# The first stage multiplies half of the GLA gate columns before the shift is known; the GLA groups run with five tiles

## The chip, the core and the metric

The kernel runs on one core of one Trainium2 chip. The metric is device time in microseconds (us), the median of several runs. Lower is better. TensorE multiplies, VectorE and ScalarE prepare its operands, GpSimd computes small reciprocal roots, SyncE (SP) issues the loads.

## What is computed

One hybrid layer for 512 tokens of width 2048, all in float32. Its six modulation rows come from the conditioning row `c`:

```python
mod = (c_act @ w_ada[i] + b_ada[i])[:, None, :]
shift_m, scale_m, gate_m, shift_f, scale_f, gate_f = jnp.split(mod, N_MOD, axis=-1)
h = rmsnorm(x, g_pre_mix[i]) * (1.0 + scale_m) + shift_m
y = token_mixer(h, ...)            # inside: proj = h @ w_in
fq, fk, fv, ff, gq, gk, gv, ga, gr = jnp.split(proj, IN_OFFSETS, axis=-1)
...
gla = head_rmsnorm(gla, g_gla_out).reshape(b, s, GLA_WIDTH) * jax.nn.silu(gr)
```

`w_in` has 2048 rows. Its columns feed eight attention heads (FoX, 128 wide, queries, keys and values), four linear-attention heads (GLA, keys 128, values 256, gate `gr` 256 wide each) and 24 small columns (`ff`, `ga`). An output projection and a squared-ReLU network of hidden width 8192 follow; the change leaves them alone.

## The kernel before

**Precision.** A float32 product is made of three fast matmuls (`split_mm`, L775): each operand is split into a rounded part (`_hi`, a copy on ScalarE) and a rest (`_lo`, a subtraction on VectorE), and hi x hi, hi x lo and lo x hi are summed in PSUM. A plain float32 matmul (L813) needs no split operands, and takes longer.

**Groups.** The input projection is cut into eight groups: four FoX groups of two heads and four GLA groups of one head. Each has `TILES` = 6 tiles of 128 output columns by 512 tokens, one PSUM bank each, and runs over KT = 16 k-tiles of 128 rows (`group_steps`, L781). The operand `h`, transposed, stays in `in_hi` and `in_lo`; in a GLA group the tiles are GQ, GK, GV0, GV1, GR0 and GR1, the last two being the two halves of the head's gate. The weights come two k-tiles at a time into two slots `w_raw`, are split into `w_hi` (L1207) and `w_lo` (L1640), and the slot's next load waits for both (`slot_free`, L503). While group r is multiplied, the small work of group r-1 is done in slots between the tiles (`fox_slot`, `gla_slot`); in four of the groups VectorE also sums the modulation columns of the second half of the layer (`f_item`, L1690). At the end of a group ScalarE copies tiles 0, 2 and 4 and VectorE tiles 1, 3 and 5 from PSUM to `grp`.

**The first stage.** Before group 0 can run, `scale_m` and `shift_m` have to be summed from 32 MB of `w_ada`. VectorE multiplies each k-row block with its `c_act` value and adds it to `am_acc` (`add_am`, L1869): 32 items of 1 MB. An item holds scale and shift columns of the same k-tiles of `h`; the table `BLOCKS` makes three blocks of four k-tiles (8 items, operations 1024 wide) and two blocks of two (4 items, 512 wide). At a block's end TensorE sums `am_acc` over the partitions with a row of ones (L981, `start_slot`), VectorE turns the sums into `mod_a` and `mod_b` (`mod_columns_m`, L1906), and ScalarE modulates the k-tile and rounds it (`modulate`, L1345: `in_tmp` L1347, `in_hi` L1350); VectorE makes `in_lo` (L1897). k-tiles 2, 3, 6 and 7 (`WHOLE`) are multiplied as plain float32, from `w_raw` and `in_tmp`. The 40 small columns (`misc_step`, L986) are multiplied at the places that `FILL_AT` names. Before all this, ScalarE squares and scales the four x tiles, TensorE transposes them (L965) and ScalarE copies them to `xn_t` (L1339).

**Queues.** Each engine works its instructions in the order in which they are written. SP issues all loads of the stage in one row (L620 to L640): four item slots, so item n waits until item n-4 is used.

**Between group 0 and 1.** The small columns give the forget gates: VectorE L1973 to L1976, ScalarE Exp and Ln with a table load (L1367, L1369), and only then ScalarE's evictions of group 0 (L1218).

Of the kernel before, what the change touches and what calls it, by code (L numbers as in the profile page):

```python
# [35 lines left out]
F32 = mybir.dt.float32  # L36
# [5 lines left out]
P = 128  # L42
# [3 lines left out]
def build_block(nc, x, c, w_ada, b_ada, g_pre_mix, g_post_mix, w_in, b_fgate, w_gla_a2, b_gla_a2,  # L46
# [30 lines left out]
    GQ, GK, GV0, GV1, GR0, GR1 = range(6)  # L77
    MM_G = KT // 2
# [19 lines left out]
    F_USED = len(ITEMS)  # L98
# [14 lines left out]
    with ExitStack() as ctx:  # L113
# [39 lines left out]
        am_item = [at(f"am_item{s}", [P, 2, 2, 512], (R_AD, R_AD + 8 * KIB, R_G, R_G + 8 * KIB)[s]) for s in range(4)]  # L153
        am_acc = [at(f"am_acc{s}", [P, 2, 512], (R_T + 12 * KIB, R_GG + 4 * KIB)[s]) for s in range(2)]
# [4 lines left out]
        wm_hi = at("wm_hi", [P, KT, 40], R_GG, F32R)  # L159
# [48 lines left out]

        acc = small("acc", [P, 2 * P])
# [16 lines left out]
        decay = small("decay", [P, NCH])  # L226
        assert k_at[0] <= nc.sbuf_usable_end
# [33 lines left out]

        hi_done = sem("hi_done")
# [8 lines left out]
        rows_tr = sem("rows_tr")  # L271
        c_tr = sem("c_tr")
        cols_ready = sem("cols_ready")
        ce_ready = sem("ce_ready")
        c_ready = sem("c_ready")
# [2184 lines left out]
```

## Time and profile before

| | |
|---|---|
| time, median of 3 runs | 2235.53 us (2233.84 to 2235.6) |
| profiled execution, span from first to last instruction | 2231.3 us |
| around the span (median less span) | 4.2 us |
| TensorE busy | 2171.6 us, 97% |
| VectorE busy | 1508.8 us, 68% |
| ScalarE busy | 868.1 us, 39% |
| GpSimd busy | 376.0 us, 17% |
| granted TensorE clock, mean | 0.993 |
| moved by DMA | 441.17 MB, mean 198 GB/s |

The profile is of one execution; its own time is the span and what lies around it, here taken from the median. A row of the timeline has the start, the duration, engine, line, operation, what it writes and reads, how often, and in brackets the idle time of the engine before it with what ended it. The durations of matmuls overlap: what counts is the distance of their starts. Records of a plain float32 matmul come in twos.

### The profile page before, as it was taken

The page shows a single profiled execution, that of the slowest core. Times are in us where ns is not written, and L with a number is a line of the kernel's source. Part 1 is how long each engine was busy: PE and PEld are TensorE (multiplying, and loading weights), DVE is VectorE, ACT ScalarE, POOL GpSimd, SP SyncE. Part 2 cuts the span into 40 slices and gives each one's busy share as a digit, 9 for nine tenths or more (in the row PEclk, how much of TensorE's full clock was granted, in tenths as well). Part 3 has the DMA queues.
Part 4 walks back from the last instruction along what each step waited for, and adds up shares of the span by engine and source line. Part 5 has one row for each costly group of instructions (what it writes and reads, how often), then busy time and mean ns, then how long its engine had stood idle before and what let it go on. Part 6 is the DMA issues. An engine that isn't in the chain of part 4 may idle for free.

```text
span 2231.3 us, 26551 instructions
## 1 busy us (share of the span) xinstructions
PE 2171.6 (97%) x9835; PEld 1765.5 (79%) x9835; DVE 1508.8 (68%) x1485; ACT 868.1 (39%) x1096; POOL 376.0 (17%) x207
## 2 busy tenths in 40 slices
PE   4989999999999999999999999999999999999998
PEld 3568888887777888888888888888878888888886
DVE  6877666666767634664355445544689889898998
ACT  5233333331333223533344335334443444343443
POOL 1000000000000001100000000000035545463645
PEclk9999999999999999999999999999999999999999
DMA  9956554753554353565666656746364765567663
GB/s 363 355 181 215 196 178 142 237 162 113 159 170 137 108 195 101 182 220 215 206 205 220 222 173 205 240 174 203 132 207 170 244 227 169 190 234 244 239 230 147
DMA packets 266403, 441.17 MB, mean 198 GB/s; under 512 B 18156, under 2 KB 118704, under 8 KB 260280
## 3 DMA queue, kind: packets, MB, share of 16 engines
q1 hardware_dynamic: 265472, 435.45, 58.1%
q10 hardware_dynamic: 824, 4.27, 0.5%
q8 instruction: 70, 1.15, 0.2%
q14 instruction: 37, 0.30, 0.0%
HBM read 379.88 MB, written 59.79 MB: 197 GB/s over the span
## 4 chain that ended last, share of the span: by engine, by line
PE 85%; issue 8%; DVE 4%; DMA 1%; ACT 1%; SPq 1%; POOL 0%; DVEq 0%; POOLq 0%; ACTq 0%
PE pair L777 27%; PE pair L779 27%; PE pair L778 26%; DVE am_acc L1880 2%; DMA am_item<-in_w_ada 1%; PE pair L886 1%; PE pair L860 1%; DVE v_op L2165 0%; PE pair L877 0%; PE pair L981 0%; PE pair L926 0%; PE pair L935 0%; PE pair L827 0%; SPq L607 0%; POOL rstd L2330 0%
## 5 line engine op out<-in xcount | busy, mean ns | idle before, releaser
L777 PE MATMUL pair<-in_hi,w_hi 128*128 128x512 f32 (+1 forms) x1800 | 719.6, 400 | 9.2 <-DVE in_lo L2073 3.8
L779 PE MATMUL pair<-in_hi,w_lo 128*128 128x512 f32 (+1 forms) x1800 | 697.2, 387 | 0.0
L778 PE MATMUL pair<-in_lo,w_hi 128*128 128x512 f32 (+1 forms) x1800 | 696.2, 387 | 0.0
L1640 DVE TENSOR_TENSOR w_lo<-w_raw,w_hi 128x2048 fp32r<-128x2048 f32 (+1 forms) x139 | 289.5, 2083 | 395.5 <-ACT w_hi L1207 395.1
L1207 ACT ACTIVATE w_hi<-w_raw 128x2048 fp32r<-128x2048 f32 (+1 forms) x141 | 243.4, 1726 | 466.1 <-PE pair L779 404.8
L777 PEld LDWEIGHTS pair<-in_hi,w_hi 128*128 128x128 f32 x1800 | 339.4, 189 | 88.6 <-issue 20.1
L779 PEld LDWEIGHTS pair<-in_hi,w_lo 128*128 128x128 f32 x1800 | 338.8, 188 | 70.2
L778 PEld LDWEIGHTS pair<-in_lo,w_hi 128*128 128x128 f32 x1800 | 339.6, 189 | 67.6 <-issue 2.6
L777 PE MATMUL pair<-v_op,hid_r 128*128 128x512 f32 x896 | 349.0, 390 | 2.1 <-issue 0.9
L779 PE MATMUL pair<-v_op,hid_r 128*128 128x512 f32 x896 | 348.6, 389 | 0.0
L778 PE MATMUL pair<-v_op,hid_r 128*128 128x512 f32 x896 | 348.6, 389 | 0.0
L2165 DVE TENSOR_TENSOR v_op<-v_raw,v_op 128x1024 fp32r<-128x1024 f32 x192 | 302.3, 1595 | 64.8 <-ACT v_op L1613 63.6
L1613 ACT ACTIVATE v_op<-v_raw 128x1024 fp32r<-128x1024 f32 x192 | 203.3, 1061 | 287.1 <-PE pair L779 269.0
L2409 POOL TENSOR_TENSOR v_sum<-v_raw,v_raw 128x512 f32<-128x512 f32 x60 | 149.2, 2513 | 364.1 <-DVE v_raw L2180 364.1
L777 PEld LDWEIGHTS pair<-v_op,hid_r 128*128 128x128 f32 x896 | 168.2, 188 | 38.9 <-issue 3.2
L779 PEld LDWEIGHTS pair<-v_op,hid_r 128*128 128x128 f32 x896 | 168.2, 188 | 34.9
L778 PEld LDWEIGHTS pair<-v_op,hid_r 128*128 128x128 f32 x896 | 168.2, 188 | 34.8
L2418 POOL TENSOR_TENSOR v_raw<-v_raw,v_sum 128x512 f32<-128x512 f32 x60 | 135.3, 2284 | 18.4 <-DVE v_op L2165 18.4
L2336 POOL TENSOR_TENSOR ada<-ada,c_act 128x2048 f32<-128x2048 f32 x8 | 29.8, 3721 | 592.3 <-DMA ada<-in_w_ada 555.0
L2215 DVE TENSOR_TENSOR y_t<-pair,y_t 128x1024 f32<-128x1024 f32 x104 | 125.0, 1215 | 0.3 <-PE pair L779 0.3
L777 PE MATMUL pair<-w_hi,in_hi 128*128 128x512 f32 x256 | 101.3, 396 | 0.0
L778 PE MATMUL pair<-w_lo,in_hi 128*128 128x512 f32 x256 | 99.7, 389 | 0.0
(218 smaller groups left out, 1928.9 us busy)
## 6 DMA issues: line engine op xcount, KB each, us to landing
w_raw<-in_w_mlp_in SPq DMA_DIRECT2D x64, 1024.0 KB, 5.3
v_raw<-in_w_mlp_out SPq DMA_DIRECT2D x128, 512.0 KB, 4.9
hid_r<-hid_scratch SPq DMA_DIRECT2D x112, 512.0 KB, 6.3
hid_scratch<-hid_r SPq DMA_DIRECT2D x28, 1792.0 KB, 7.9
am_item<-in_w_ada SPq DMA_DIRECT2D x64, 512.0 KB, 7.6
w_raw<-in_w_in SPq DMA_DIRECT2D x128, 256.0 KB, 3.5
af_item<-in_w_ada SPq DMA_DIRECT2D x64, 512.0 KB, 4.5
w_raw<-in_w_in SPq DMA_DIRECT2D x128, 128.0 KB, 3.6
```

The source lines that it names most:

```text
L777: pe.matmul(dst, a[0], b[0], start=start, stop=False, skip_group_check=onto)
L778: pe.matmul(dst, a[0], b[1], start=False, stop=False, skip_group_check=onto)
L779: return pe.matmul(dst, a[1], b[0], start=False, stop=stop, skip_group_check=onto)
L1207: act.activation(w_hi[n][:, view], w_raw[n][:, view], ACT.Copy).then_inc(hi_done, 1)
L1613: act.activation(v_op[i % 4][:, 0, :], raw_of(u, p)[:, h, :], ACT.Copy).then_inc(v_hi, 1)
L1640: dve.tensor_tensor(w_lo[n][:, view], w_raw[n][:, view], w_hi[n][:, view].bitcast(F32), ALU.subtract)\
L1880: last = dve.scalar_tensor_tensor(total, item, c_k, total, ALU.mult, ALU.add)
L2165: dve.tensor_tensor(v_op[i % 4][:, 1, :], raw_of(u, p)[:, h, :], v_op[i % 4][:, 0, :].bitcast(F32), ALU.subtract).then_inc(v_lo, 1)
L2215: return dve.tensor_tensor(dst, src[:, :, :], dst, ALU.add)
L2336: pool.tensor_tensor(unit[:, :, :], unit[:, :, :], c_act[:, :].rearrange("p (k o) -> p k o", o=1).to_broadcast([P, KT, P]), ALU.mult)\
L2409: last = pool.tensor_tensor(v_sum[:, h, cols], v_raw[q[B22]][:, h, cols], v_raw[q[B11]][:, h, cols], ALU.add)
L2418: last = pool.tensor_tensor(b21, b21, v_sum[:, h, cols], ALU.subtract)
```

## The change

The 128 columns of GR1 of all four GLA heads (512 columns of `w_in`) are taken out of the GLA groups, which then have `GLA_TILES` = 5 tiles. They are multiplied in the first stage, as four plain float32 tiles per k-tile, from `in_tmp` = `xn_t` times `mod_a` alone, that is with the scale and without the shift (`fill_operand`, `fill_w`). The results are parked in `gg`. The shift's share is the same for all tokens: the sum over k of `mod_b` times the weight. For this the same columns are loaded again in the four FoX groups, four k-tiles in each (`load_gr`), VectorE sums them into `gr_acc` (`gr_step`), and TensorE makes the column sums at the end of the last FoX group (`f_columns` with `gates`). When a GLA group is evicted, VectorE adds the parked tile and this column (`evict_gla`).

So the items are cut otherwise: first 16 items of the scale, then 16 of the shift, each with four k-rows of 512 columns, so that all operations are 512 wide. The k-tiles in plain float32 are gone from group 0, and so is `FILL_AT`: the small columns follow the tiles of their k-tile. The x tiles are loaded before the first item.

```diff
+    GLA_TILES = TILES - 1
...
-    BLOCKS = ((0, 4), (4, 4), (8, 4), (12, 2), (14, 2))
-    M_BLOCKS = len(BLOCKS)
-    ITEMS = [(b, i) for b, (_, nk) in enumerate(BLOCKS) for i in range(2 * nk)]
+    S_BLOCKS = KT // 4
+    M_BLOCKS = 2 * S_BLOCKS
...
             def load_am(n):
                 if n >= 4:
                     sp.wait_ge(am_used, n - 3)
+                block, i = divmod(n, 4)
+                col = (SCALE_M, SHIFT_M)[block // S_BLOCKS] + block % S_BLOCKS * 512
+                for half in range(2):
+                    k = 4 * i + 2 * half
+                    sp.dma_start(am_item[n % 4][:, 2 * half:2 * half + 2, :], w_ada_t[:, k:k + 2, col:col + 512])\
                         .then_inc(am_in[n % 4], 16)
...
+            for t in range(TB):
+                load_x(t)
+            for n in range(16):
                 load_am(n)
+                if n % 2 == 0:
+                    load_fill(n // 2)
             load_fox(0, 0, wait=False)
+            load_wm(0)
+            for n in range(16, 20):
+                load_am(n)
             load_fox(0, 1, wait=False)
+            load_wm(1)
...
+            for n in range(20, 32):
                 load_am(n)
+                if n % 2 and n < 28:
+                    load_fox(0, (n - 17) // 2)
...
+                    if mm == 1:
+                        load_gr(r - 1)
```

TensorE:

```diff
+            for k in range(KT):
+                if k % 4 == 0:
+                    sum_columns(k // 4)
+                    pe.wait_ge(fill_in[k // 4], 64)
+                pe.wait_ge(fill_tmp, k + 1)
+                for h in range(GLA_HEADS):
+                    last = pe.matmul(bank[h][:, :], fill_w[k // 2][:, k % 2, h, :], in_tmp[:, k, :],
+                                     start=(k == 0), stop=(k == KT - 1))
+                    if k == KT - 1 or k % 2 and h == GLA_HEADS - 1:
+                        last.then_inc(fill_used, 1)
+            sum_columns(S_BLOCKS)
+
+            SUM_AT = {7: S_BLOCKS + 1, 14: S_BLOCKS + 2, 22: S_BLOCKS + 3}
...
-            group_steps(FOX_GROUPS, False, fox_slots(FOX_GROUPS - 1))
+            group_steps(FOX_GROUPS, False, fox_slots(FOX_GROUPS - 1, gates=True), GLA_TILES)
             with pe.Fori(0, GLA_HEADS - 1) as h:
-                group_steps(h + (FOX_GROUPS + 1), False, lambda s: gla_slot(s, h))
+                group_steps(h + (FOX_GROUPS + 1), False, lambda s: gla_slot(s, h), GLA_TILES)
```

ScalarE:

```diff
+            for k in range(KT):
+                fill_operand(k)
             first_hi(0)
+            gate_hi(0)
+            for h in range(GLA_HEADS):
+                act.wait_ge(fill_used, MM_G + h)
+                act.activation(gg[:, h * 512:h * 512 + 512], bank[h][:, :], ACT.Copy).then_inc(fill_park, 1)
             for k in range(KT):
                 modulate(k)
+                if k == 1:
+                    first_hi(1)
+                    gate_hi(1)
+                elif k % 2 and k < KT - 1:
+                    split_hi((k + 1) // 2, arrived_group(0, (k + 1) // 2), (k + 1) // 2 % 2, group_view)
```

VectorE:

```diff
+            for block in range(S_BLOCKS):
+                for i in range(4):
+                    add_am(4 * block + i)
+                mod_columns(block)
+            first_lo(0)
+            add_am(16)
+            gate_lo(0)
+            for n in range(17, 20):
+                add_am(n)
+            mod_columns(S_BLOCKS)
...
+            for block in range(1, S_BLOCKS):
+                n, k = 4 * (S_BLOCKS + block), 4 * block
+                if block == 1:
+                    add_am(n)
+                    add_am(n + 1)
+                split_lo(2 * block, 0, group_view)
+                add_am(n + 2)
+                add_am(n + 3)
+                mod_columns(S_BLOCKS + block)
+                modulated_lo(k)
+                modulated_lo(k + 1)
+                split_lo(2 * block + 1, 1, group_view)
+                if block + 1 < S_BLOCKS:
+                    add_am(n + 4)
+                modulated_lo(k + 2)
+                modulated_lo(k + 3)
+                if block + 1 < S_BLOCKS:
+                    add_am(n + 5)
...
+            def gr_step(f, j):
+                dve.drain()
+                if j == 0:
+                    dve.wait_ge(gr_in, f * 64 + 64)
+                dve.scalar_tensor_tensor(gr_acc[:, :], gr_item[:, j, :], mod_b[:, bass.ds(f * 4 + j, 1)], gr_acc[:, :],
+                                         ALU.mult, ALU.add).then_inc(gr_used, 1)
...
+                    if b == GR1:
+                        dve.wait_ge(fill_park, GLA_HEADS)
+                        dve.tensor_scalar(grp[:, b, :], gg[:, bass.ds(h * 512, 512)], v_col[:, bass.ds(h, 1)], None,
+                                          ALU.add).then_inc(ev_dve, 1)
```

The order of TensorE's row behind the transposes of x, in the kernel before: the column sums (`ones,am_acc`), then the first k-tile in three parts.

```order
L965 MATMUL pair<-ident,x_raw 128x128 x3
L981 MATMUL pair<-ones,am_acc_86 128x1 [waits am_used,xt_act]
L981 MATMUL pair<-ones,am_acc_86 128x1 x7
L777 MATMUL pair<-in_hi,w_hi_76 128x512 [waits mod_lo,lo_done,hi_done]
L778 MATMUL pair<-in_lo,w_hi_76 128x512
L779 MATMUL pair<-in_hi,w_lo_78 128x512
```

The same place in the changed kernel, to the second of eight sums.

```order
L978 MATMUL pair<-ones,am_acc_86 128x1 [waits am_used,xt_act]
L978 MATMUL pair<-ones,am_acc_86 128x1 x3
L989 MATMUL pair<-in_tmp,fill_w_88 128x512 [waits fill_tmp,fill_in0]
L989 MATMUL pair<-in_tmp,fill_w_88 128x512 x3
L989 MATMUL pair<-in_tmp,fill_w_88 128x512 [waits fill_tmp]
L989 MATMUL pair<-in_tmp,fill_w_88 128x512 x3
...
L978 MATMUL pair<-ones,am_acc_87 128x1 [waits am_col,am_used]
L978 MATMUL pair<-ones,am_acc_87 128x1 x3
```

Where the split matmuls began, 16 plain tiles now stand, then the next sum; the split matmuls begin behind the fifth sum.

VectorE's row from the sum of one shift block to the next, in the changed kernel (`am_acc` sums of items, `w_lo` and `in_lo` rests).

```order
L1977 TENSOR_TENSOR mod_b<-pair,cols_a 128x4 [waits am_sum]
L1949 TENSOR_TENSOR in_lo<-in_tmp,in_hi 128x512 [waits mod_hi] x2
L1673 TENSOR_TENSOR w_lo_79<-w_raw_75,w_hi_77 128x1536 [waits w_used,hi_done]
L1936 TENSOR_SCALAR am_acc_86<-am_item_82,c_act 128x512 [waits am_sum,am_in0]
L1934 SCALAR_TENSOR_TENSOR am_acc_86<-am_item_82,c_act,am_acc_86 128x512 x3
L1949 TENSOR_TENSOR in_lo<-in_tmp,in_hi 128x512 [waits mod_hi] x2
L1934 SCALAR_TENSOR_TENSOR am_acc_86<-am_item_83,c_act,am_acc_86 128x512 [waits am_in1]
L1934 SCALAR_TENSOR_TENSOR am_acc_86<-am_item_83,c_act,am_acc_86 128x512 x3
L1673 TENSOR_TENSOR w_lo_78<-w_raw_74,w_hi_76 128x1536 [waits w_used,hi_done]
```

Behind these come two more items and the wait for the next sum. All item operations are now 512 wide, and both w_lo of a block stand between two sums.

TensorE's row at the last k-tile of group 0, before: the 40 small columns (`wm_hi`) ahead of the six tiles, of which the first is shown.

```order
L777 MATMUL pair<-in_hi,wm_hi 40x512 [waits mod_lo]
L778 MATMUL pair<-in_lo,wm_hi 40x512
L779 MATMUL pair<-in_hi,wm_lo 40x512
L777 MATMUL pair<-in_hi,w_hi_77 128x512
L778 MATMUL pair<-in_lo,w_hi_77 128x512
L779 MATMUL pair<-in_hi,w_lo_79 128x512
```

And in the changed kernel: the last tile, the small columns, and the first tile of group 1.

```order
L790 MATMUL pair<-in_hi,w_hi_77 128x512
L791 MATMUL pair<-in_lo,w_hi_77 128x512
L792 MATMUL pair<-in_hi,w_lo_79 128x512
L790 MATMUL pair<-in_hi,wm_hi 40x512
L791 MATMUL pair<-in_lo,wm_hi 40x512
L792 MATMUL pair<-in_hi,wm_lo 40x512
L790 MATMUL pair<-in_hi,w_hi_76 128x512 [waits ev_act,lo_done,hi_done]
```

The small columns have moved from before the six tiles to behind them.

## Rows read from the trace of the kernel before

**Rows 1.** The page, part 1: busy us (share of the span), instructions.

```profile
PE 2171.6 (97%) x9835; PEld 1765.5 (79%) x9835; DVE 1508.8 (68%) x1485; ACT 868.1 (39%) x1096; POOL 376.0 (17%) x207
```

**Rows 2.** Stretches: length, busy us of each engine, TensorE's granted clock, DMA share, GB/s.

```profile
40.00:50.00 10.00, 7.08 (x22) 5.81 (x22) 7.50 (x10) 5.46 (x8) 0.00 (x0) 0.51 1.09 359
60.00:70.00 10.00, 5.83 (x16) 2.37 (x14) 6.82 (x6) 1.84 (x2) 0.00 (x0) 1.00 1.08 355
200.00:220.00 20.00, 20.00 (x96) 16.05 (x95) 14.74 (x35) 6.88 (x12) 1.10 (x2) 1.00 0.57 184
520.00:540.00 20.00, 20.00 (x96) 15.90 (x96) 16.91 (x25) 3.58 (x3) 1.02 (x1) 1.00 0.28 79
```

**Rows 3.** Timeline of TensorE: start, duration, line, operation, [idle before].

```profile
27.37 9.79 PE L965 MATMUL pair<-ident,x_raw 128*128 128x128 f32 x64 [16.21 <-ACT x_raw L1327]
38.71 2.80 PE L981 MATMUL pair<-ones,am_acc 128*128 128x1 f32 x16 [1.55 <-DVE am_acc L1880]
44.43 0.76 PE L777 MATMUL pair<-in_hi,w_hi 128*128 128x512 f32 x1 [2.92 <-DVE in_lo L1897]
...
55.18 10.46 PE L813 MATMUL pair<-in_tmp,w_raw 128*128 128x512 f32 x24
69.81 3.20 PE L981 MATMUL pair<-ones,am_acc 128*128 128x1 f32 x16 [4.17 <-DVE am_acc L1880]
...
103.00 0.47 PE L777 MATMUL pair<-in_hi,w_hi 128*128 128x512 f32 x1 [0.81 <-DVE in_lo L1897]
...
137.78 0.95 PE L981 MATMUL pair<-ones,am_acc 128*128 128x1 f32 x8
...
142.31 0.40 PE L777 MATMUL pair<-in_hi,w_hi 128*128 128x512 f32 x1
...
146.42 0.40 PE L777 MATMUL pair<-in_hi,wm_hi 128*40 128x512 f32 x1
...
147.11 0.39 PE L777 MATMUL pair<-in_hi,w_hi 128*128 128x512 f32 x1
```

**Rows 4.** Timeline of VectorE in the first stage, the same columns.

```profile
22.23 16.33 DVE L1880 SCALAR_TENSOR_TENSOR am_acc<-am_item,c_act,am_acc 128x1024 f32<-128x1024 f32 x12 [4.50 <-DMA am_item<-in_w_ada]
...
102.17 0.68 DVE L1897 TENSOR_TENSOR in_lo<-in_tmp,in_hi 128x512 fp32r<-128x512 f32 x1
...
111.12 1.75 DVE L1640 TENSOR_TENSOR w_lo<-w_raw,w_hi 128x1536 fp32r<-128x1536 f32 x1
...
117.32 0.48 DVE L1882 TENSOR_SCALAR am_acc<-am_item,c_act 128x512 f32<-128x512 f32 x1
117.88 2.40 DVE L1880 SCALAR_TENSOR_TENSOR am_acc<-am_item,c_act,am_acc 128x512 f32<-128x512 f32 x3
```

**Rows 5.** Timeline of ScalarE in the first stage.

```profile
6.43 0.18 ACT L1322 ACTIVATE c_act<-pair 128x16 f32<-128x16 f32 x1
...
16.97 1.91 ACT L1333 ACTIVATE x_junk<-x_raw 128x2048 f32<-128x2048 f32 x1 [1.27 <-DMA x_raw<-in_x]
...
100.59 0.81 ACT L1347 ACTIVATE in_tmp<-xn_t,mod_b,mod_a 128x512 f32<-128x512 f32 x1 [10.58 <-DVE mod_a L1918]
```

**Rows 6.** Timeline from group 0 to group 1, three engines.

```profile
147.31 0.74 DVE L1973 TENSOR_SCALAR f_z<-pair,b_fg 8x512 f32<-8x512 f32 x1 [0.40 <-PE pair L779]
...
152.18 1.58 ACT L1218 ACTIVATE grp<-pair 128x512 f32<-128x512 f32 x3
...
152.92 0.47 PE L777 MATMUL pair<-in_hi,w_hi 128*128 128x512 f32 x1 [1.54 <-ACT grp L1218]
```

**Rows 7.** Waits of TensorE from 140 to 820 us: all there are.

```profile
PE pair L777 <- ACT grp L1218: 1.5, 1, 1.5
```

**Rows 8.** Timeline at a GLA group's start: its second pair of weights.

```profile
558.10 1.49 ACT L1207 ACTIVATE w_hi<-w_raw 128x1536 fp32r<-128x1536 f32 x1 [5.80 <-DMA w_raw<-in_w_in]
...
559.62 1.76 DVE L1640 TENSOR_TENSOR w_lo<-w_raw,w_hi 128x1536 fp32r<-128x1536 f32 x1 [2.51 <-ACT w_hi L1207]
...
562.45 0.48 PE L777 MATMUL pair<-in_hi,w_hi 128*128 128x512 f32 x1
```

More of the change, by code:

```diff
@@ L260, in build_block @@
         out_done = sem("out_done")
+        fill_in = [sem(f"fill_in{b}") for b in range(S_BLOCKS)]
+        fill_tmp = sem("fill_tmp")
+        fill_used = sem("fill_used")
+        fill_park = sem("fill_park")
+        gr_in = sem("gr_in")
+        gr_used = sem("gr_used")
         hi_done = sem("hi_done")
@@ L640, in _ @@
-            load_fox(0, MM_G - 1, first=True)
+                if n % 2 and n < 28:
+                    load_fox(0, (n - 17) // 2)
+            for mm in range(6, MM_G):
+                load_fox(0, mm)
             def load_cumb(f):
@@ L779, in split_mm, with group_steps @@
                 return pe.matmul(dst, a[1], b[0], start=False, stop=stop, skip_group_check=onto)
-            def group_steps(r, first, slot, misc_step=None):
+            def group_steps(r, first, slot, tiles, misc_step=None):
                 for k in range(KT):
@@ L804, in group_steps @@
-                    for b in range(TILES):
-                        if k == 0 and not first:
+                        pe.wait_ge(mod_lo, k + 1)
+                    for b in range(tiles):
+                        if k == 0 and first and b < GLA_HEADS:
+                            pe.wait_ge(fill_park, b + 1)
+                        elif k == 0 and not first:
                             pe.wait_ge((ev_act, ev_dve)[b % 2], r * 3 - 2 + b // 2)
                         cols = slice(b * P, b * P + P)
-                        if by_parts:
-                            last = split_mm(bank[b][:, :], (hi[:, cols], lo[:, cols]),
-                                            (in_hi[:, k, :], in_lo[:, k, :]), k == 0, k == KT - 1)
-                        else:
-                            last = pe.matmul(bank[b][:, :], raw[:, cols], in_tmp[:, k, :], start=False, stop=False)
-                        if k == KT - 1 and b < TILES - 1:
+                        last = split_mm(bank[b][:, :], (hi[:, cols], lo[:, cols]),
+                                        (in_hi[:, k, :], in_lo[:, k, :]), k == 0, k == KT - 1)
+                        if k == KT - 1 and b < tiles - 1:
@@ L824, in f_columns @@
+                    if first:
+                        misc_step(k)
+                    else:
+                        slot(2 * k + 1)
+            def f_columns(f, gates=False):
+                if gates:
+                    pe.wait_ge(gr_used, KT)
+                    for h in range(GLA_HEADS):
+                        pe.matmul(BA[:, 8 + h:9 + h], gr_acc[:, h * P:h * P + P], ones[:, 0:1], start=True, stop=True)
                 pe.wait_ge(am_used, f * F_ITEMS + (F_USED + F_ITEMS))
@@ L1389, in _, with group @@
             CAT_AT = {4 * (k // 2 + 1) + 2 + k % 2: k for k in range(12)}
-            def group(r, work, last=False):
+            def group(r, work, view, last=False):
                 for s in range(4 * MM_G):
@@ L1875, in add_am @@
                     dve.wait_ge(am_sum, block - 1)
-                for k in range(ks.start, ks.stop):
-                    item, c_k = item_view(n)[:, k - ks.start, :, :], c_act[:, k:k + 1]
-                    if k:
+                for j in range(4):
+                    item, c_k = am_item[n % 4][:, j, :], c_act[:, 4 * i + j:4 * i + j + 1]
+                    if i or j:
                         dve.drain()
@@ L1994, in _, with group @@
             CAT_AT = {4 * (k // 2 + 1) + 2 + k % 2: k for k in range(12)}
-            def group(r, work, last=False):
+            def group(r, work, view, last=False):
                 for s in range(4 * MM_G):
```

434 lines of the change are left out of this document (190 added, 244 removed).

## The prediction

> **What bounds the kernel now.** I read the page's busy times first, then stretches of 10 and 20 us, then the first 160 us engine by engine, then the waits behind them. TensorE is busy 97% of the span [rows 1], and from 200 to 220 us in every microsecond at full clock [rows 2]. After the first stage the trace shows one wait of TensorE up to 820 us, 1.5 us long [rows 7]. So every matmul taken out of the head groups is worth its full spacing, unless the shorter group uncovers a wait. The first stage is different: the DMA engines are full there (share 1.08 to 1.09, some 355 GB/s), TensorE is busy 5.8 of 10 us in one stretch [rows 2], and it waits for column sums that VectorE has to finish first (4.17 us in front of the sum at 69.81) [rows 3]. The stage ends where group 1 starts, at 152.92 us [rows 6].
>
> **Prices.** One k-step of six tiles in three parts (18 matmuls) goes from 142.31 to 146.42: 4.11 us, 0.685 a tile; the 40-column step beside it takes 0.69, so a step of the first stage costs 4.80 [rows 3]. A full-precision tile: two k-steps are 12 tiles, which the trace shows as 24 records in 10.46 us, 0.872 a tile [rows 3]. A four-column sum takes 0.95 at full clock and, by half of the 3.20 for eight, 1.6 at half clock [rows 3]; I take 1.8 with its start. VectorE: a 1024-wide product-sum has a pitch of 1.36 (12 in 16.33), a 512-wide one 0.82 (3 in 2.40), the first of a block 0.48 plus a gap; a w_lo 1.75, an in_lo 0.68 [rows 4]. So an item of 1 MB costs 2.7 us in the old form and 3.3 (3.0 for the first of a block) in the new one: 32 items take about 104 us where 20 wide and 12 narrow ones took 92. ScalarE: 0.81 for a modulation [rows 5], and less for the rounding copy behind it.
>
> The Trainium skill ("VectorE: DVE Perf Modes", the errata section) says that each instruction pays a fixed extra, and that tiles of 512 elements or more hide it. An estimate by its add formula makes four 512-wide operations 0.3 us dearer than two 1024-wide ones; the rows say 0.6. By the page the stage would lose half as much to the narrower items.
>
> **The first stage, step by step.**
> 1. Start. The x tiles go ahead of the items. The third x tile, now the third MB instead of the fifth, no longer makes ScalarE wait at 16.97; its eight passes of 1.9 to 2.0 us then run without a gap from 6.6, behind its first operation [rows 5]. The transposes start near 23.0 instead of 27.37, and the first sum, 11.3 us after them as now [rows 3], at 34.3. Gain 4.4. Items 0 to 3 are summed by about 31.6.
> 2. The fill. Four blocks, each: sum 0.95, VectorE's columns and ScalarE's operand about 1.35 (0.47 and 0.81, and hand-overs), then 16 full-precision tiles, 13.95. A block takes 16.25; four take 65.0, to 99.3. VectorE works 12.9 of each 16.25 us and then stands at its wait for the sum, so it can't run ahead.
> 3. The hand-over to the shift half. VectorE is let go by the fourth sum at about 84.5. Next in its row is the first w_lo, and ScalarE copies w_hi only behind four fill operands: 88.9. Then 1.7 for w_lo, 0.45 for the gate part, 13.0 for items 16 to 19: 104.0. TensorE has waited 4.7 us. Sum 1.8, shift columns 0.2, modulation, in_lo: the first split matmul starts at about 108.3 (44.43 now).
> 4. Sixteen k-steps of 4.80: 76.8. Whole k-tiles are gone: four k-steps fall from 5.23 to 4.11. Three sums, 5.4.
> 5. Waits in that half. Between two sums VectorE has four items (13.0), two w_lo (3.5), four in_lo (2.7), 19.4 in all, and stands idle for the sum and modulation after each sum (about 3.4), and for a w_hi that waits until TensorE has released the slot (1 to 3.4). That is 24 to 27 us a block against TensorE's 20.1. Walked through in order, TensorE waits 4.4, 4.5 and 4.5 us at the three sums: 13.4. The wait of this kind at 69.81 now is 4.17 [rows 3].
> 6. Clock. After 2.92 us of idling the first matmuls run at half clock (granted 0.51 from 40 to 50 us) for about 5 us; after 0.81 and 1.54 us of idling the next matmul takes 0.47 and then full pace holds [rows 2, 3, 6]. So the 1.35 us gaps of the fill cost no clock, and the waits of steps 3 and 5 do, four times; what isn't swallowed by the next wait on VectorE is about 4.5. The last matmul of the stage ends near 208.4: 108.3 + 76.8 + 5.4 + 13.4 + 4.5.
> 7. To group 1. The gate part of k = 15 now stands behind the tiles instead of ahead of them. From VectorE's f_z at 147.31 to group 1 takes 5.6 us (f_z, copy, minimum, Exp, table load, Ln, first eviction), of which TensorE now sees 1.54 [rows 6]. It will see all 5.6, and a restart at half clock, 2.3: group 1 at full pace from 216.3, against 152.9. **The stage costs 63.4 us.**
>
> The DMA isn't the bound any more: 4.2 MB more in the stage, but 25 MB are wanted by 84 us, at 355 GB/s 70.
>
> The Trainium skill ("FP8 and Floating Point Precision", TensorE Precision Notes) says that true FP32 takes 4 passes, against the 3 parts of this kernel's split. That speaks against multiplying the gate columns in this form: an estimate from four passes at this trace's spacing of 0.228 us is 58.4 us for the 64 tiles. By the rows it is 55.8; the trace nearly agrees, and the sum would be 2.6 us worse by the page.
>
> **The groups.** Four GLA groups lose one tile in each of 16 k-steps: 64 x 0.685 = 43.8 us gained, because nothing waits there [rows 7]. Against it:
> - Group start. w_hi of the second pair starts at 558.10, w_lo at 559.62, ready at 561.38; TensorE needs it at 562.45, 1.07 us later [rows 8]. TensorE gets there 1.37 us sooner, the eviction that releases SP's queue comes 0.68 us later relative to the start, the copies are 0.5 us shorter. About 0.4 in each of three groups: 1 us; bounds 0 and 4.
> - The tile from the fill costs an addition on VectorE where a copy stood: nothing, eight tiles of cover are left.
> - Four 0.82 us gr_steps and four small loads (2 us of SP's queue) in each of four fox groups: VectorE is busy 14.7 of 20 us there [rows 2] and the next w_raw has several us in hand. Taken as 1 in all, bounds 0 and 4. The four column sums at the end: 1.
>
> Sum: 63.4 - 43.8 + 3 = 22.6 us. Span 2231.3 + 22.6 = 2253.9; the kernel's time stands 4.2 above its span (median 2235.5), so **2258 us**, 1.0% slower. Likeliest case's own range: 2246 to 2268, from the clock cost absent and waits 1 us shorter each to the bounds of the groups.
>
> **Rivals.**
> - TensorE is the only pacer. VectorE's own work in a block of the second half, 19.4 us, is less than TensorE's 20.1; if the queues let it run ahead, no sum waits. Then: first split matmul at 102.7 (steps 1 and 2, a sum, 2.4), + 76.8 + 2.9 + 5.6 = 188.0, the stage costs 35.1, the groups give 43.8 with nothing against it: 8.7 us faster, 2227. It decides as soon as VectorE's loop between two sums is under 20.1 us. For it: 97% busy TensorE nearly everywhere. Against it: VectorE's row has the wait for each sum behind all four items, and TensorE's row the sum ahead of the k-step that would cover it. Chance 0.09.
> - Half of the waits hide and the clock holds: 2238 to 2246. Chance 0.12.
> - The five-tile groups become VectorE's. It is busy 16.9 of 20 us from 520 to 540 [rows 2]; one sixth less time there leaves 16.7. A lag of 3 us in each of four groups gives 2270. Against it: w_lo is narrower by a sixth, and the busy stretch is one in four. Chance 0.09.
> - The change doesn't save what it says, because the shift's share or the second pass over the weights sits on TensorE's path: only 4 tiny matmuls and 16 VectorE steps are added, so 0.02, above 2270.
>
> **How the numbers follow.** Forecast 0.68, 2258. The range 2238 to 2270 leaves out the first rival and the upper tails. A measurement of this kernel tells 0.2% (4.5 us) from no change. Faster: the first rival, 0.09. Same: the low edge of the second, 0.03. Slower: the rest, 0.88.
>
> **What would show it.** Right if, in the profile after, the first sum stands near 34, the fill's 64 tiles take 56 us in four blocks of 14 with gaps of about 1.4, the first split matmul comes near 108, TensorE waits for am_acc before each of the sums at about 104, 129, 155 and 181 by 4 to 5 us, group 1 starts near 214 after a wait of over 5 us for ScalarE's eviction, and the GLA groups follow each other at 64 instead of 75 us. Wrong if the stage ends before 195, or if a GLA group takes over 67.

## The result and the profile after

The changed kernel takes 2268.03 us (median of 4 runs, 2265.43 to 2269.14), the kernel before 2235.51 in the same session: ratio 1.0147, interval 1.0135 to 1.0159, so 1.5% slower. The forecast was 2258 with a range up to 2270: the side and most of the mechanism were right, the loss was 10 us too small. The profiled execution took 2265.43 us, its span is 2263.6: it is the fastest of the four, 2.6 us under the median. In all runs with both figures the time stands 1.8 us above the span, not the 4.2 that the table of before gives, so the profile of before is a fast execution too (about 2233.1), and the two spans compare fairly: they differ by 32.3 us, the medians by 32.5.

The page's busy times hardly differ from [rows 1]: TensorE still stands at 97%.

```profile
PE 2188.9 (97%) x9807; PEld 1762.7 (78%) x9807; DVE 1525.7 (67%) x1550; ACT 876.5 (39%) x1118; POOL 374.8 (17%) x207
```

TensorE's timeline of the first stage, the changed kernel (L978 are the column sums, L989 the fill, L790 the first part of a split matmul; to compare with [rows 3, 6]):

```profile
23.53 8.53 PE L969 MATMUL pair<-ident,x_raw 128*128 128x128 f32 x64 [11.93 <-ACT x_raw L1347]
33.41 1.05 PE L978 MATMUL pair<-ones,am_acc 128*128 128x1 f32 x8 [1.35 <-ACT xn_t L1359]
35.80 15.67 PE L989 MATMUL pair<-in_tmp,fill_w 128*128 128x512 f32 x32 [1.33 <-ACT in_tmp L1363]
...
71.38 13.97 PE L989 MATMUL pair<-in_tmp,fill_w 128*128 128x512 f32 x32 [1.34 <-ACT in_tmp L1363]
...
105.62 1.05 PE L978 MATMUL pair<-ones,am_acc 128*128 128x1 f32 x8 [2.48 <-DVE am_acc L1934]
109.36 0.77 PE L790 MATMUL pair<-in_hi,w_hi 128*128 128x512 f32 x1 [2.69 <-DVE in_lo L1949]
131.25 1.12 PE L978 MATMUL pair<-ones,am_acc 128*128 128x1 f32 x8 [2.57 <-DVE am_acc L1934]
155.75 1.67 PE L978 MATMUL pair<-ones,am_acc 128*128 128x1 f32 x8 [4.56 <-DVE am_acc L1934]
183.89 1.87 PE L978 MATMUL pair<-ones,am_acc 128*128 128x1 f32 x8 [4.60 <-DVE am_acc L1934]
...
217.62 0.77 PE L790 MATMUL pair<-in_hi,w_hi 128*128 128x512 f32 x1 [5.64 <-ACT grp L1230]
```

Group 1 starts at 217.62 us instead of 152.92, **64.7 us later**. Stretches of the same kernel, with the granted clock as the third number from the end (columns as in [rows 2]):

```profile
35.00:40.00 5.00, 4.20 (x6) 1.83 (x7) 4.54 (x7) 2.49 (x4) 0.00 (x0) 0.66 1.10 351
75.00:80.00 5.00, 5.00 (x13) 2.17 (x12) 4.54 (x7) 0.00 (x0) 0.00 (x0) 1.00 0.88 286
185.00:190.00 5.00, 5.00 (x14) 4.06 (x15) 1.55 (x3) 2.78 (x4) 0.00 (x0) 0.50 0.09 33
215.00:220.00 5.00, 2.38 (x6) 1.93 (x7) 3.34 (x5) 3.42 (x5) 0.00 (x0) 0.50 0.03 7
```

VectorE in the same stage shows the other side of TensorE's waits: it stands before w_lo until ScalarE has made w_hi, and before each column until TensorE has summed it.

```profile
86.17 0.16 DVE L1973 TENSOR_TENSOR mod_a<-pair,cols_a 128x4 f32<-128x4 f32 x1 [2.82 <-PE pair L978]
...
90.57 1.76 DVE L1955 TENSOR_TENSOR w_lo<-w_raw,w_hi 128x1536 fp32r<-128x1536 f32 x1 [4.00 <-ACT w_hi L1368]
...
165.83 1.76 DVE L1673 TENSOR_TENSOR w_lo<-w_raw,w_hi 128x1536 fp32r<-128x1536 f32 x1 [4.61 <-ACT w_hi L1219]
...
212.02 0.74 DVE L2018 TENSOR_SCALAR f_z<-pair,b_fg 8x512 f32<-8x512 f32 x1 [6.95 <-PE pair L792]
```

The GLA groups are best timed by the matmul that opens each one's gate work. In the kernel before these stand 74.94, 74.94 and 74.26 us apart; the last three of the four:

```profile
554.31 1.12 PE L906 MATMUL pair<-ga_t,a2h 16*128 16x512 f32 x2
629.25 1.12 PE L906 MATMUL pair<-ga_t,a2h 16*128 16x512 f32 x2
703.51 0.69 PE L906 MATMUL pair<-ga_t,a2h 16*128 16x512 f32 x1
```

In the changed kernel 64.07, 65.56 and 66.67:

```profile
539.51 0.69 PE L910 MATMUL pair<-ga_t,a2h 16*128 16x512 f32 x1
603.58 0.69 PE L910 MATMUL pair<-ga_t,a2h 16*128 16x512 f32 x1
669.14 0.69 PE L910 MATMUL pair<-ga_t,a2h 16*128 16x512 f32 x1
735.81 0.69 PE L910 MATMUL pair<-ga_t,a2h 16*128 16x512 f32 x1
```

They gain 10.9, 9.4 and 7.6 us, not 10.95 (16 tiles of 0.685) each. The last row stands 32.3 us behind that of before: +64.7 at group 1's start, +2.1 in group 1 (its restart at half clock and a wait of 0.5 for prob), -34.5 in the four five-tile groups (6.7 in the one that carries the last FoX slots, 27.8 in the other three); the rest of the kernel adds nothing (the spans differ by 32.3 too). TensorE's waits from 140 to 820 us, where the kernel before has one line [rows 7]:

```profile
PE pair L978 <- DVE am_acc L1934: 9.2, 2, 4.6
PE pair L790 <- ACT grp L1230: 5.6, 1, 5.6
PE pair L790 <- DVE w_lo L1673: 2.4, 3, 1.8
PE pair L881 <- ACT prob L1279: 1.9, 3, 0.8
PE pair L920 <- DVE g_e L1864: 1.6, 2, 0.8
PE pair L899 <- DVE f_o L1825: 0.2, 1, 0.2
```

### The profile page after: what moved, and what is told of

Its sections match the earlier page's. It is cut to its first block, busy times and chain, and to the rows that moved or that the text cites. A ratio compares the mean times of both kernels' runs of the same rounds, so it can differ in the third digit from the quotient of the medians.

```text
span 2263.6 us, 26717 instructions
## 1 busy us (share of the span) xinstructions
PE 2188.9 (97%) x9807; PEld 1762.7 (78%) x9807; DVE 1525.7 (67%) x1550; ACT 876.5 (39%) x1118; POOL 374.8 (17%) x207
## 4 chain that ended last, share of the span: by engine, by line
PE 80%; issue 8%; DVE 5%; ACT 2%; DMA 1%; DVEq 1%; SPq 1%; POOL 0%; ACTq 0%; POOLq 0%
PE pair L790 25%; PE pair L792 25%; PE pair L791 25%; PE pair L989 2%; DVE am_acc L1934 1%; DMA w_raw<-in_w_in 1%; PE pair L890 1%; PE pair L864 1%; DVE w_lo L1673 1%; DVE v_op L2210 0%; ACT w_hi L1219 0%; PE pair L978 0%; PE pair L881 0%; ACT x_junk L1353 0%; ACT x_raw L1347 0%
## 5 line engine op out<-in xcount | busy, mean ns | idle before, releaser
L790 PE MATMUL pair<-in_hi,w_hi 128*128 128x512 f32 (+1 forms) x1760 | 707.4, 402 | 14.7 <-ACT grp L1230 5.6
L792 PE MATMUL pair<-in_hi,w_lo 128*128 128x512 f32 (+1 forms) x1760 | 683.7, 388 | 0.0
L791 PE MATMUL pair<-in_lo,w_hi 128*128 128x512 f32 (+1 forms) x1760 | 682.9, 388 | 0.0
L1673 DVE TENSOR_TENSOR w_lo<-w_raw,w_hi 128x2048 fp32r<-128x2048 f32 (+2 forms) x142 | 286.4, 2017 | 404.1 <-ACT w_hi L1219 403.6
L1219 ACT ACTIVATE w_hi<-w_raw 128x2048 fp32r<-128x2048 f32 (+2 forms) x142 | 238.4, 1679 | 448.8 <-PE pair L792 417.9
L790 PEld LDWEIGHTS pair<-in_hi,w_hi 128*128 128x128 f32 x1760 | 333.6, 190 | 93.2 <-issue 25.0
L792 PEld LDWEIGHTS pair<-in_hi,w_lo 128*128 128x128 f32 x1760 | 332.8, 189 | 69.5
L791 PEld LDWEIGHTS pair<-in_lo,w_hi 128*128 128x128 f32 x1760 | 334.0, 190 | 66.6 <-issue 2.6
L790 PE MATMUL pair<-v_op,hid_r 128*128 128x512 f32 x896 | 349.1, 390 | 2.1 <-issue 0.9
L790 PEld LDWEIGHTS pair<-v_op,hid_r 128*128 128x128 f32 x896 | 168.2, 188 | 39.0 <-issue 3.2
L2413 POOL TENSOR_TENSOR f_r<-f_ms,neg_half 128x1 f32<-128x1 f32 x32 | 23.1, 723 | 489.0 <-DVE f_ms L1816 489.0
L790 PE MATMUL pair<-w_hi,in_hi 128*128 128x512 f32 x256 | 101.2, 395 | 0.0
```

Of the source, the lines that this page charges most:

```text
L790: pe.matmul(dst, a[0], b[0], start=start, stop=False, skip_group_check=onto)
L791: pe.matmul(dst, a[0], b[1], start=False, stop=False, skip_group_check=onto)
L792: return pe.matmul(dst, a[1], b[0], start=False, stop=stop, skip_group_check=onto)
L1219: act.activation(view(w_hi[n]), view(w_raw[n]), ACT.Copy).then_inc(hi_done, 1)
L1673: dve.tensor_tensor(view(w_lo[n]), view(w_raw[n]), view(w_hi[n]).bitcast(F32), ALU.subtract)\
```

## The experiments

Nine kernels, each timed against the kernel before (medians of 2234.8 to 2235.5 in its sessions). e1 and e4 leave a part of the layer out; the others compute all of it. My theory had three parts: the five-tile groups lose to waits of their own (e1), the stage is paced by engines that wait for each other in turn and not by anyone's load (e2 to e6), and the start gains only because blocks are small (e9). e7 and e8 follow from what the others showed.

| kernel | us | range | runs | ratio to before, interval |
|---|---|---|---|---|
| e1 five tiles alone | 2199.92 | 2198.58 to 2202.15 | 4 | 0.984 (0.9824 to 0.9857) |
| e2 small columns first | 2265.99 | 2263.94 to 2267.26 | 4 | 1.0137 (1.012 to 1.0154) |
| e3 sums early | 2263.54 | 2262.21 to 2264.79 | 4 | 1.0125 (1.0108 to 1.0142) |
| e4 a third of the fill | 2264.24 | 2259.64 to 2265.17 | 4 | 1.0123 (1.0107 to 1.014) |
| e5 VectorE's order | 2257.5 | 2253.95 to 2259.13 | 4 | 1.0095 (1.0079 to 1.0112) |
| e6 all orders | 2240.41 | 2238.12 to 2245.09 | 10 | 1.0023 (1.0014 to 1.0033) |
| e7 order in the GLA groups | 2237.29 | 2235.77 to 2242.29 | 10 | 1.0013 (1.0004 to 1.0022) |
| e8 items in pieces | 2231.42 | 2227.74 to 2234.01 | 11 | 0.9982 (0.9973 to 0.9991) |
| e9 x first, before | 2235.89 | 2234.85 to 2236.73 | 10 | 1.0004 (0.9994 to 1.0014) |

**e1: the groups without the stage.** The kernel before, its GLA groups cut to five tiles:

```diff
-                    for b in range(TILES):
+                    for b in range(tiles):
...
-            group_steps(FOX_GROUPS, False, fox_slots(FOX_GROUPS - 1))
+            group_steps(FOX_GROUPS, False, fox_slots(FOX_GROUPS - 1), GLA_TILES)
```

> The kernel before with one edit: the GLA groups multiply five tiles, and the tile GR1 is left out of the computation altogether (no fill, no share of the shift; its eviction copies old sums). Theory: what the five-tile groups lose against 4 x 10.9 us is their own, waits for w_lo, prob and g_e that six tiles had covered, and not the work on gr_acc and v_col. Then the three GLA groups that begin here save about what they saved in the changed kernel (10.9, 9.4, 7.6 us) and the group that carries the last FoX slots 6.7 to 7.5: 2235.5 - 34.6 to 35.4 = 2200 to 2201 us. Rival: the added gate work is what delays them, and alone they save 4 x 10.9 = 43.8 us: 2191.7 us.

2199.92 us, 35.6 less than before: the theory's number, 8 us from the rival's. Here no VectorE step of the gates is added, and the groups show the same distances (64.05 and 65.48 us, for 64.07 and 65.56) and the same waits, 1.8 for w_lo and twice 0.8 for g_e (the third distance is 68.48 for 66.67, since the clock falls behind the 1.8 here):

```profile
PE pair L790 <- DVE w_lo L2022: 2.0, 2, 1.8
PE pair L929 <- DVE g_e L1832: 1.6, 2, 0.8
```

So the work on `gr_acc` and `v_col` is close to free (8.2 us of the 43.8 are missing here, 9.3 in the changed kernel), and the shorter group itself uncovers the waits.

**e4: does the fill set the pace of its half?** Most of its matmuls left out:

```diff
-                for h in range(GLA_HEADS):
+                for h in range(GLA_HEADS if k in (0, KT - 1) else 1):
...
-                    if k == KT - 1 or k % 2 and h == GLA_HEADS - 1:
+                    if k == KT - 1 or k % 2:
```

> The changed kernel with 42 of its 64 fill matmuls left out (of the 16 k-steps only 0 and 15 multiply all four heads' gate columns, the others one head's), so most of the half of the gate tiles is missing from the output. Theory: in the fill half TensorE does not set the pace; without 42 x 0.872 = 36.6 us of its work the blocks are still 13.1 (VectorE's 16 operations) + about 2.2 (sum, mod_a and the way back) = 15.2 to 16 us apart instead of 17.9, so it is only 6 to 8 us faster in all: 2260 to 2262 us. Rival: the stage is bound by TensorE and all its work counts: -25 to -36 us, 2232 to 2243 us.

2264.24: 36.6 us of TensorE's work are gone, and the time falls by 3.8, far from the rival's 25 and less than the 6 to 8 expected. The sums now stand 15.23 us apart, and TensorE waits for VectorE before each of them:

```profile
48.12 1.86 PE L978 MATMUL pair<-ones,am_acc 128*128 128x1 f32 x8 [4.47 <-DVE am_acc L1934]
...
63.35 1.87 PE L978 MATMUL pair<-ones,am_acc 128*128 128x1 f32 x8 [5.53 <-DVE am_acc L1934]
```

The distance is what the theory says, so the fill as such costs little there; what the stage pays for is a block's round: 13.1 us of VectorE and the way over TensorE and ScalarE and back. The gain at the fifth sum is 5.7 us (99.92 for 105.62), at group 1 it is 3.6 (214.05 for 217.62): the mean granted clock of this execution is 0.980, against 0.990 in the changed kernel, which fits that a part of what the missing work gave went to the clock.

**e3: take the gap out of that round.** The next sum goes two tiles ahead of the block's end:

```diff
+                if k == 0:
+                    sum_columns(0)
                 if k % 4 == 0:
-                    sum_columns(k // 4)
...
+                    if h == 2 and k % 4 == 3 and k < KT - 1:
+                        sum_columns(k // 4 + 1)
```

> The changed kernel with one edit: the sum of the next scale block is issued two tiles before the end of the running fill block, so the fill need not stand still while the column goes to VectorE, ScalarE and back. Theory: the four gaps of 1.33 us go and with them the half clock behind three of them (15.67 instead of 13.97 us); a block then takes about 15.0 us of TensorE (13.97 and a sum of 1.0) and about as much of VectorE, and sum 5 comes at 99 to 100 us instead of 105.62, since VectorE still stands 4 us before w_lo: -5.5 to -6.5 us, 2261.5 to 2262.5 us; granted clock 0.95 or more from 40 to 90 us. Rival: VectorE's 16 operations, not the handover, pace a block, and the sum placed early only moves the wait into the block: sums still 17 to 18 us apart, under -2 us.

2263.54, 4.5 less, where 5.5 to 6.5 were expected. One gap is left, the first, and behind it the clock still falls (28 records of the fill take 15.03 us at 36.96). The sums at 51.83, 66.46 and 81.08 are 14.6 us apart instead of 16.1 to 17.9. Then the 4 us before w_lo stand in the way: sum 5 waits 3.92 for VectorE.

```profile
81.08 0.95 PE L978 MATMUL pair<-ones,am_acc 128*128 128x1 f32 x8
...
101.51 1.87 PE L978 MATMUL pair<-ones,am_acc 128*128 128x1 f32 x8 [3.92 <-DVE am_acc L1937]
```

**e2: the end of the stage.** The small columns of k = 15 go ahead of the six tiles:

```diff
+                        if k == KT - 1:
+                            misc_step(k)
                     for b in range(tiles):
...
-                    if first:
+                    if first and k < KT - 1:
                         misc_step(k)
-                    else:
+                    elif not first:
```

> The changed kernel with one edit: the last small-column step (k = 15) stands ahead of the six tiles of that step instead of behind them. Theory: group 1 starts late because the chain f_z, Exp, Ln, first eviction begins only when the last matmul has ended; with the small columns 12 us earlier the 5.64 us wait falls to the 1.5 us of the kernel before, and with it the half clock at the start of group 1 (about 2 us): -4 to -6.2 us, 2262 to 2264 us, group 1's first matmul 4.1 us earlier. Rival: another wait comes in its place (w_hi or w_lo of the step after, or tile 0's eviction on ScalarE): -1 to -2 us, 2266 to 2267 us.

2265.99, 2.0 less; by the times alone this is unclear, since the intervals overlap, and it is the rival's number, not the theory's 4 to 6.2. In the profile the hand-over does what was expected: the wait is 1.54 and the matmul behind it takes 0.47 instead of 0.77. From the last sum (187.13) to group 1 it is 29.6 us against 33.7.

```profile
216.69 0.47 PE L790 MATMUL pair<-in_hi,w_hi 128*128 128x512 f32 x1 [1.54 <-ACT grp L1232]
```

Ahead of the last sum this execution stands 3.2 us later than the changed kernel's, which has to do with the clock and not with the edit: the fill starts at 37.04 for 35.80 and its first block takes 16.94 for 15.67. Group 1 then takes 80.8 us for 79.7 to the column sums at its end, though its start at half clock is gone: its waits for prob, prob_t and w_lo sum to 2.4 us, against 0.5. So the hand-over gains its 4.1 us and the rival's other waits take a part of them.

**e5: VectorE's order.** An item ahead of each w_lo that has to be waited for:

```diff
-            first_lo(0)
             add_am(16)
+            first_lo(0)
...
-                split_lo(2 * block, 0, group_view)
                 add_am(n + 2)
+                split_lo(2 * block, 0, group_view)
...
-                split_lo(2 * block + 1, 1, group_view)
                 if block + 1 < S_BLOCKS:
                     add_am(n + 4)
+                split_lo(2 * block + 1, 1, group_view)
```

> The changed kernel with one edit: on VectorE the next pair of ada operations on an item stands ahead of the split w_lo that waits for ScalarE (item 16 ahead of the first w_lo, item n+2 ahead of w_lo(2b), item n+4 ahead of w_lo(2b+1)). Theory: in the shift half TensorE and VectorE wait for each other in turn: TensorE stands 4.6 us at a sum because VectorE stood 4.0 to 4.6 us before a w_lo (rows at 90.57, 165.83), whose w_hi waits for the k-step that TensorE has queued behind that sum. With the items ahead of the wait sum 5 comes 2.4 us earlier, sums 6 to 8 another 1.3, 2 and 4 us: -8 to -11 us, 2257 to 2260 us. Rival: DMA paces the items (DMA share 1.0 to 1.1 from 20 to 90 us), the VectorE waits only move to the items: under -3 us, 2265 us or more.

2257.5, 10.5 less, as the theory says and not as the rival on DMA does (under 3). The waits at sums 6 to 8 fall from 2.57, 4.56 and 4.60 to these:

```profile
129.89 1.05 PE L978 MATMUL pair<-ones,am_acc 128*128 128x1 f32 x8 [1.27 <-DVE am_acc L1934]
152.19 1.65 PE L978 MATMUL pair<-ones,am_acc 128*128 128x1 f32 x8 [2.38 <-DVE am_acc L1934]
177.39 1.05 PE L978 MATMUL pair<-ones,am_acc 128*128 128x1 f32 x8 [1.65 <-DVE am_acc L1934]
```

**e6: all of it.** Besides e2, e3 and e5:

```diff
             for k in range(KT):
+                if k == KT - 4:
+                    first_hi(0)
+                    gate_hi(0)
                 fill_operand(k)
-            first_hi(0)
-            gate_hi(0)
...
-            SUM_AT = {7: S_BLOCKS + 1, 14: S_BLOCKS + 2, 22: S_BLOCKS + 3}
+            SUM_AT = {7: S_BLOCKS + 1, 15: S_BLOCKS + 2, 23: S_BLOCKS + 3}
```

> The changed kernel with the edits of e2_misc_first, e3_sums_early and e5_vector_order together, w_hi(0) on ScalarE ahead of the last four fill operands, and the sums 7 and 8 three tiles later (behind the third tile of k = 7 and of k = 11). Theory: the work is the same, only the waits between the engines go: sum 5 at about 96 us, sums 6 to 8 about 23 us apart (VectorE: 13.1 of items, 3.5 of w_lo, 2.8 of in_lo, the rest the way over TensorE and ScalarE), group 1 starts at 190 to 194 us instead of 217.6: -22 to -27 us, 2241 to 2246 us, which takes back most of the loss but not all. Rival: DMA becomes the pace at once (51 MB of the stage at the 350 to 370 GB/s of its first half are 140 to 147 us, behind which stand the last four k-steps), or the new orders bring new waits: -12 us or less, 2256 us or more.

2240.41, 27.6 less than the changed kernel, with the same work done; 22 to 27 were expected, 12 or less by the rival. Sum 5 stands at 95.04, the others 22.3 to 24.3 us apart, group 1 at 192.01.

```profile
95.04 1.05 PE L980 MATMUL pair<-ones,am_acc 128*128 128x1 f32 x8 [0.26 <-DVE am_acc L1940]
...
192.01 0.47 PE L790 MATMUL pair<-in_hi,w_hi 128*128 128x512 f32 x1 [1.54 <-ACT grp L1235]
```

**e7 and e8: the remaining waits.** e7, in the GLA groups (`lo_first` is slot 24):

```diff
-            G_AT = {s: divmod(n, 2) for n, s in enumerate((2, 5, 9, 11, 15, 17, 19, 23))}
+            G_AT = {s: divmod(n, 2) for n, s in enumerate((2, 6, 9, 11, 15, 17, 19, 23))}
...
+                    if s in lo_first:
+                        split_lo(r * MM_G + (s // 4 + 1), (s // 4 + 1) % 2, view)
                     work(s)
```

> The kernel of e6_all_orders with the order of VectorE in the five-tile GLA groups mended in two places: the item of the gate row that stands ahead of g_e (slot 5) goes one slot later, and the eighth w_lo stands ahead of cat's row in slot 24. Theory: the waits that a five-tile group shows (0.84 and 0.77 us for g_e, 1.84 us for w_lo) are VectorE's order and not its load, so they go: -3 to -3.5 us, 2237 to 2237.5 us. Rival: VectorE is full there (4.8 of 5 us busy in stretches), another of its operations becomes late in their place: under -1 us, 2239.5 us or more.

2237.29, 3.1 less, as expected: both g_e waits are gone, and the w_lo wait of 1.84 has fallen to 1.00.

```profile
697.88 0.47 PE L790 MATMUL pair<-in_hi,w_hi 128*128 128x512 f32 x1 [1.00 <-DVE w_lo L1679]
```

e8 on top of it, in the shift half:

```diff
+                if more:
+                    add_am(n + 4, (0, 1))
                 modulated_lo(k)
+                if more:
+                    add_am(n + 4, (2,))
                 modulated_lo(k + 1)
+                if more:
+                    add_am(n + 4, (3,))
                 split_lo(2 * block + 1, 1, group_view)
-                if block + 1 < S_BLOCKS:
-                    add_am(n + 4)
```

> The kernel of e7_gate_order, and in the shift half an item's four operations are spread over the gaps in which VectorE waits for ScalarE's in_hi (two ahead of the first in_lo of a block, one behind each of the first two). Theory: VectorE stands 1.5 + 0.7 + 0.7 us behind each mod_b, and TensorE's waits at the sums (2.3, 0.5, 1.9 us in e6) come from it: they nearly go, -3 to -4.5 us more than e7, 2233 to 2234.5 us, which is 0.5 to 2 us under the kernel before. Rival: in_lo comes later by what is put ahead of it, TensorE waits for it at the first k-step instead: no gain over e7, 2237 us.

2231.42, 5.9 less than e7 and more than expected; **0.18% under the kernel before** (interval 0.09 to 0.27%), and so the fastest kernel here that computes everything. The sums hardly wait any longer, 0.6 us in all where those of e7 waited 3.4:

```profile
160.40 1.05 PE L980 MATMUL pair<-ones,am_acc 128*128 128x1 f32 x8 [0.31 <-DVE am_acc L1941]
185.08 0.47 PE L790 MATMUL pair<-in_hi,w_hi 128*128 128x512 f32 x1 [1.54 <-ACT grp L1235]
```

**e9: the start alone.** The kernel before with the four x tiles ahead of the first two items.

> The kernel before with one part of the change: the four x tiles are loaded ahead of the first two ada items. Theory: the transposes start 4 us earlier, as in the changed kernel (27.37 to 23.5 us), but the first sum waits for VectorE's 16 operations of 1024 columns (ready at 38.6 us now, later by what the items wait behind x), so the stage gains nothing and loses up to 2 us: 2235 to 2238 us. Rival: the start is TensorE's and ScalarE's chain of x: -3 to -4 us, 2231.5 us.

2235.89, against 2234.80 of the kernel before: no change, as the theory says. The transposes start 2.9 us earlier, and the sum waits 5.47 for VectorE where it waited 1.55 [rows 3].

```profile
24.49 9.18 PE L963 MATMUL pair<-ident,x_raw 128*128 128x128 f32 x64 [12.91 <-ACT x_raw L1325]
39.15 3.55 PE L979 MATMUL pair<-ones,am_acc 128*128 128x1 f32 x16 [5.47 <-DVE am_acc L1878]
```

## Why the prediction was right, and where it was off

Most of the mechanism held, the size less: 2268.03 lies at the very top of the likeliest case's own range, 2246 to 2268. In the stage two misses pulled against each other, which is luck; in the groups nothing offset the miss.

- **Step 1, the start:** right; 23.53 and 33.41 for 23.0 and 34.3. e9 shows that x first gives nothing by itself; that the change's smaller first block is what lets it gain fits this, but was not tried alone.
- **Steps 2 and 6, the fill and the clock:** step 6 failed where it says that "the 1.35 us gaps of the fill cost no clock". The gaps are 1.33, but three of the four blocks behind them fell to half clock and took 15.67 instead of 13.97 us: 5.1 us. Part of it is hidden behind VectorE's wait for w_lo: TensorE waits 2.48 us at the fifth sum, where 4.7 were forecast. e3, which takes away three of the gaps and the falls behind them, is 4.5 us faster.
- **Step 3, the hand-over:** right in kind. VectorE stands 4.0 before w_lo; the first split matmul comes at 109.36 for 108.3.
- **Steps 4 and 5, the shift half:** right in kind and nearly in size. The waits are 2.57, 4.56 and 4.60 for 4.4, 4.5 and 4.5. e5 shows that they come from the order on VectorE. From 109.36 to the last small column, at 211.8, are 102.4 us: 76.8 for k-steps, 4.7 for sums, 11.7 for waits, and 9.2 left for the clock, about 2.3 for each of four restarts. Step 6 put 4.5, what the next wait on VectorE doesn't swallow; but the waits came out only 1.7 shorter than forecast. This is the mis-sized term of the stage.
- **Step 7, to group 1:** right; the wait is 5.64 for 5.6. Group 1 starts at 217.62, the stage with its restart costs 64.7 + 2.1 = 66.8 us for 63.4.
- **The groups:** the larger miss. 43.8 less 3 was predicted, 34.5 measured. The step that failed is "43.8 us gained, because nothing waits there [rows 7]". Rows of a six-tile group can't tell what a five-tile group waits for. The "Group start" item looked at the second pair of weights, and the waits came elsewhere, each for a step that stands behind something else in VectorE's row: g_e behind an item of the gate row, w_lo behind a row of `cat` (the next operand), and prob, for which ScalarE stands idle 4.30 us, waits for neg_max behind items of the layer's second half. The waits sum to 5.6 us, the gate columns (L829) cost 1.

```profile
475.37 0.40 ACT L1279 ACTIVATE prob<-logit,neg_max 128x128 f32<-128x128 f32 x1 [4.30 <-DVE neg_max L1803]
```

Most of the other 2.7 us (an estimate from a few rows) is how a wait is counted: from the modelled end of the matmul before it, which lies behind the next one's start. By starts, g_e's transposes follow the last matmul after 0.23 us where nothing waits (the first two rows) and after 1.22 where the idle time says 0.84 (the others), and the tile behind them comes 0.07 later too. Eight such waits make some 1.5 us. In two of the groups the transposes of the values (L915) are late by 0.5 and 0.2 us as well, too little to be listed as idle time.

```profile
553.00 0.39 PE L792 MATMUL pair<-in_hi,w_lo 128*128 128x512 f32 x1
553.23 0.60 PE L920 MATMUL pair<-ident,g_e 128*128 128x128 f32 x4
...
617.51 0.39 PE L792 MATMUL pair<-in_hi,w_lo 128*128 128x512 f32 x1
618.73 0.66 PE L920 MATMUL pair<-ident,g_e 128*128 128x128 f32 x4 [0.84 <-DVE g_e L1864]
```

e1 shows that the loss isn't the added work, e7 that a third of it is two places in VectorE's order. It is the rival on VectorE, at three quarters of its 12 us; that part at least is order and not load.

- **Rival "TensorE is the only pacer":** fell in this kernel (e4), yet e8 comes near it. Its sums stand 20.6 to 21.6 us apart, for the 20.1 that the rival names, and the stage is nearly TensorE's: 148.2 us from the first fill to group 1, of which 139.3 are work (55.8 + 76.8 + 7 sums of 0.95).
- **The other rivals:** half of the waits hidden with the clock held fell, since all the forecast waits are there and the clock did fall. The fourth fell too: the gate columns at the end cost 0.9 us (the next tile starts 2.60 us behind the first of the 24 records, before 1.71 behind the first of 16).
- **DMA:** not the bound, as predicted, but near it: VectorE waits 2.2 us in all for items between 20 and 200 us, while e6 finds the share at 1.06 to 1.10 in six of seven stretches of 10 us from 20 to 90.
- **Slips in the working:** the kernel before has 24 wide and 8 narrow items, not 20 and 12 (its total of 92 us is about right), and VectorE's own work between two sums adds up to 19.2 us, not 19.4. Neither moves the forecast.

The change's limit follows from its prices. The fill adds 64 x 0.872 = 55.8 us of TensorE and takes 43.8 away, 12 more in all. Against that it can win what TensorE stood idle in the stage before, the 14.8 us of these two rows and the 1.5 of [rows 7], with some 4 at the start and 4.5 for whole k-tiles no longer multiplied in full precision:

```profile
PE pair L981 <- DVE am_acc L1880: 11.1, 3, 5.4
PE pair L777 <- DVE in_lo L1897: 3.7, 2, 2.9
```

That makes about 13 us, of which e8 gets 3.6. It is an estimate without the clock: a stage without waits could also win back what the kernel before loses at half clock (granted 0.51 from 40 to 50 us [rows 2]).

## What to carry to other kernels

Work that is moved into an idle stage is worth only as much as that stage's idle time, and only if the engines that feed it don't wait for each other in turn; here the order in the queues was worth 27.6 us, and 36.6 with the last two steps, more than the 13 that the change could gain by the estimate above. Where an in-order engine has to wait, put independent work ahead of the wait, in pieces as small as the gap. Before counting a shortened loop at its full saving, look at what stands just ahead of each producing step in its engine's queue: the slack that the longer loop gave it is what goes.

## What was unexpected in the hardware

- The same gap costs the clock in one execution and not in another. Behind the gap of 1.34 us in front of the fill, 28 records of 14 tiles took 12.25 us in e6 and 15.15 in e8, the same instructions in the same order. In the kernel before, gaps of 0.81 and 1.54 kept the clock. The rows of e6 and then of e8:

```profile
36.50 12.25 PE L994 MATMUL pair<-in_tmp,fill_w 128*128 128x512 f32 x28 [1.34 <-ACT in_tmp L1368]
```

```profile
36.93 15.15 PE L994 MATMUL pair<-in_tmp,fill_w 128*128 128x512 f32 x28 [1.34 <-ACT in_tmp L1368]
```

- Behind a row of one-column matmuls the clock can fall without any gap. At the end of the group that carries the last FoX slots TensorE runs 24 records of them (L829, L833) in 2.6 us. In e3 the clock then falls to 0.52; in the changed kernel's profile, at the same place, it stays at 1.00. Of the eight profiles that have these 24 records, six show the fall (e3 to e8); behind the 16 records that end the other FoX groups, in 1.7 us, none does. The stretch behind them in e3, and then in the changed kernel:

```profile
534.00:536.00 2.00, 2.00 (x7) 1.50 (x6) 1.57 (x4) 0.60 (x1) 0.00 (x0) 0.52 1.06 375
```

```profile
536.00:538.00 2.00, 2.00 (x10) 1.59 (x10) 1.93 (x8) 0.57 (x1) 0.00 (x0) 1.00 1.04 387
```

- The spread is wider with it: the kernel before lies within 3.1 us over 21 runs, e6 within 7.0 over 10, from 2238.12 at a mean granted clock of 0.996 to 2245.09 at 0.993. The profile of one execution can be 3 us off its kernel's median: the changed kernel's is 2.6 under it, e6's 3.0 above. So two profiles are best compared by the intervals inside them.
